# A diagonal state-space mixer that keeps its state at every fourth step, with its matrices made one mixer ahead

## The reference, cut to what matters

```python
u, q, k, v, r, glow = split(x @ w_in)            # x: 256 x 1024
# S5: 32 groups of 16 channels, 64 complex states each = 2048 states
abar = exp((lam_re + i*lam_im) * dt)             # one complex number a state
bbar = coef(abar) * b                            # 64 x 16 a group
x[t] = abar * x[t-1] + bbar @ u[t]               # linear scan over 256 steps
y    = Re(c @ x) + d_skip * u
g    = gelu(y);  y_s5 = g * sigmoid(g @ glu_w + glu_b)
# GLA: 4 heads, chunks of 64 tokens, q_dec, k_inv, k_end, three chunk states
o    = head_norm(att @ v + q_dec @ state) * silu(r)
out  = concat(y_s5, o) @ w_out
```

## Time and profile before

| | us |
|---|---|
| median of 3 runs | 1386.54 (1384.82 to 1388.08) |
| time of the profiled execution | 1389.13 |
| its span | 1387.4 |
| PE busy in the span | 1313.1 |
| DVE busy | 582.8 |
| POOL busy | 133.8 |
| second mixer, first useful matmul (L723) to end of its last (L631) | 673.36 to 862.58 |

### The profile page before, as it was taken

One profiled execution on the slowest core, in us unless ns is written; L12 is line 12 of the kernel. 1 busy time (PEld: TensorE's weight loads), 2 busy tenths in 40 slices (PEclk: granted clock), 3 DMA queues, 4 the chain that ended last, 5 costly groups with the idle time before them and its releaser, 6 DMA issues. The chain is left out here.

```text
span 1387.4 us, 16354 instructions
## 1 busy us (share of the span) xinstructions
PE 1313.1 (95%) x6324; PEld 700.8 (51%) x6324; DVE 582.8 (42%) x1145; ACT 192.0 (14%) x317; POOL 133.8 (10%) x123
## 2 busy tenths in 40 slices
PE   7999999999999999999956779999999999999997
PEld 5864645445445445454743444645445445445443
DVE  4235623333333333333778963523333333333334
ACT  3130201111111111111120120211111111111111
POOL 1000100000000000000777830100000000000000
PEclk9999999999999999999977869999999999999999
DMA  6525949999999999997311017789999999999992
GB/s 195 164 94 204 408 169 409 422 422 422 422 422 422 422 422 421 422 422 287 110 53 61 31 61 281 304 331 418 422 421 422 422 421 422 422 422 422 422 421 84
DMA packets 75547, 448.87 MB, mean 324 GB/s; under 512 B 9456, under 2 KB 10496, under 8 KB 25600
## 3 DMA queue, kind: packets, MB, share of 16 engines
q1 hardware_dynamic: 75520, 448.52, 79.5%
HBM read 447.44 MB, written 1.05 MB: 323 GB/s over the span
## 5 line engine op out<-in xcount | busy, mean ns | idle before, releaser
L1030 PE MATMUL bank<-expert_weights,hiddenT 128*64 128x512 f32 x1024 | 233.8, 598 | 0.0
L1003 PE MATMUL bank<-expert_weights,hT 128*64 128x512 f32 x1024 | 225.3, 592 | 0.0
L1003 PE MATMUL bank<-expert_weights,weight_ring 128*64 128x512 f32 x1024 | 225.2, 592 | 0.0
L1699 DVE TENSOR_TENSOR hidden<-silu_gate,bank 128x256 f32<-128x256 f32 x64 | 27.0, 421 | 333.3 <-ACT silu_gate L1206 333.3
L1003 PEld LDWEIGHTS bank<-expert_weights,hT 128*64 128x64 f32 x1024 | 73.4, 137 | 146.6 <-issue 146.6
L1003 PEld LDWEIGHTS bank<-expert_weights,weight_ring 128*64 128x64 f32 x1024 | 73.6, 137 | 146.2 <-issue 146.2
L956 PE MATMUL bank<-onehot_r,h_top 128*128 128x256 f32 x544 | 134.1, 289 | 0.0
L1030 PEld LDWEIGHTS bank<-expert_weights,hiddenT 128*64 128x64 f32 x1024 | 67.8, 136 | 117.7 <-issue 109.6
L956 PE MATMUL bank<-onehot_r,h_low 128*128 128x256 f32 x544 | 127.1, 277 | 0.0
L937 PE MATMUL bank<-y_top,onehotT_r 128*128 128x512 f32 x264 | 111.8, 423 | 0.0
L937 PE MATMUL bank<-y_low,onehotT_r 128*128 128x512 f32 x264 | 104.5, 396 | 0.0
(11 more groups left out here) (322 smaller groups left out, 1236.3 us busy)
## 6 DMA issues: line engine op xcount, KB each, us to landing
expert_weights<-in_exp_w_gate SPq DMA_DIRECT2D x128, 1024.0 KB, 10.9
expert_weights<-in_exp_w_up SPq DMA_DIRECT2D x128, 1024.0 KB, 13.3
expert_weights<-in_exp_w_down SPq DMA_DIRECT2D x128, 1024.0 KB, 12.6
weight_ring<-in_w_in_even SPq DMA_DIRECT2D x6, 2048.0 KB, 10.2
weight_ring<-in_w_out SPq DMA_DIRECT2D x4, 2048.0 KB, 7.4
weight_ring<-in_w_in_odd SPq DMA_DIRECT2D x4, 2048.0 KB, 9.4
ln_w<-in_ln_w SPq DMA_DIRECT2D x4, 512.0 KB, 13.4
ln_b<-in_ln_b SPq DMA_DIRECT2D x4, 512.0 KB, 14.6
```

What stands on the lines that cost most here:

```text
L1003: last = nc.tensor.matmul(bank[6][a * CAP:(a + 1) * CAP, :].rearrange("p (w f) -> p w f", w=2), xq[:, c, s0:s0 + CAP], ew_gu(2 * u + a, c) ...
L1030: last = nc.tensor.matmul(bank[b][a * CAP:(a + 1) * CAP, :], hm[:, j, a * CAP:(a + 1) * CAP], ew_d(2 * u + a)[:, j, half * 512:(half + 1) ...
L1699: nc.vector.tensor_tensor(hslot[:, :], sg[:, :], bank[6][:, DE:2 * DE], ALU.mult)\
```

## The change

S5 works with four phases. For each state the kernel keeps the state only at steps 3, 7, 11, ..., that is 64 of 256, and advances it by the fourth power of `abar`. The inputs of four steps enter a state through matrices `bbar * abar^k`, k = 0 to 3 (`bt`); the outputs at the steps between leave it through `c * abar^k` (`cmat`); what an input does to outputs fewer than four steps later goes through small matrices made by `pe_direct` from `bbar` and `cmat` (`direct`). The parts:

- In `mix0`: `dve_s5_powers` (30 small operations on 128x16 data) and `pool_s5` (six doublings to 64 steps, then `bbar`), one more transpose `G` on TensorE with a copy on ScalarE, a store of `G` to memory, four loads that spread its rows over 32 partitions each, `dve_s5_matrices` (12 operations of 1024 elements, 1 of 512 and 6 of 1536), and two stores of 2 MB and 3 MB (`s5_b`, `s5_c`).
- On SyncE's queue in `mix0` the loads `q0`, `v0`, `gb0` now stand behind the store of `G` and the four spreading loads, and `o0` behind the two stores.
- In `mix1`: `s5_c` (3 MB) and `s5_b` (2 MB) are loaded. The first waits only for the first of `moe0`'s four last accumulations. `pe_direct` takes the place of the second `keep_clock`. The inputs are 128 matmuls of 32x128 weights on 64 columns, then `qk`, `v`; VectorE does all tiles at once on 64 steps; then 24 direct matmuls and 128 output matmuls of 128x32 weights on 64 columns. GpSimd has only memsets and the mask.
- The order behind: `att`, keys, `r` half, `U`, `r` half, gate, `o`, output projection `a` (S5), head transposes, projection `b` (GLA).
- `moe1` may load three experts ahead (before: one), behind the same wait for `o1`.

```diff
-            for name in ("xb0", "k0", "q0", "v0", "gb0", "o0", "out_b0", "out_a0"):
+            for name in ("xb0", "k0"):
                 ring_load(sp, ring_no[name])
+            for dst, src in ((s5_room[:, 6144:7168], A["c_odd"]), (s5_room[:, 4096:5120], A["bt_odd"]),
+                             (xg[...], A["b_odd"])):
+                sp.dma_start(dst, src).then_inc(M1["raw_in"], 16)
+            sp.wait_ge(*B0.read("G"))
+            sp.dma_start(A["s5_rows"], hslot[:, P:2 * P]).then_inc(M1["rows"], 16)
+            sp.wait_ge(M1["rows"], 16)
+            for j in range(4):
+                src = A["s5_rows"].rearrange("(a j q) s -> j a (q s)", j=4, q=4)[j]
+                sp.dma_start(s5_room[32 * j:32 * j + 32, 0:4096].rearrange("p (a n) -> p a n", a=8),
+                             src.partition_broadcast(32)).then_inc(M1["rows"], 16)
+            for name in ("q0", "v0", "gb0"):
+                ring_load(sp, ring_no[name])
+            sp.wait_ge(M1["bt"], 2)
+            sp.dma_start(A["s5_b"], s5_room[:, 0:4096]).then_inc(M1["stored"], 16)
+            sp.wait_ge(M1["tables"], 1)
+            sp.wait_ge(M1["ct"], 1)
+            sp.dma_start(A["s5_c"], s5_room[:, 6144:12288]).then_inc(M1["stored"], 16)
+            for name in ("o0", "out_b0", "out_a0"):
...
 # TensorE, mix1
+            for q in range(4):
+                for w in range(2):
+                    for r in range(4):
+                        for j in range(4):
+                            rows = slice(32 * j, 32 * j + 32)
+                            last = nc.tensor.matmul(B.tile(f"bu{j}")[:, (2 * q + w) * S5C:(2 * q + w + 1) * S5C],
+                                                    W["bt"][rows, 3 - r, w, q, :], phases[rows, q, r, :],
+                                                    start=(r == 0), stop=(r == 3))
...
+            pe.wait_ge(M1["states"], 1)
+            for q in range(4):
+                out = ...
+                for r in range(4):
+                    k, lag = (0, 0) if r == 3 else (r + 1, 1)
+                    for w in range(2):
+                        for j in range(4):
+                            last = nc.tensor.matmul(out[32 * j:32 * j + 32, r, lag:], W["cmat"][:, k, w, 4 * j + q, :],
+                                                    W["m1"][:, w, 4 * j + q, 0:S5C - lag], start=False, ...)
...
 # VectorE, mix1: in place of 16 scan_tile
+            for j in range(4):
+                nc.vector.tensor_tensor(W["m1"][:, :, 4 * j:4 * j + 4, :], bu, c, ALU.mult)
+                nc.vector.tensor_tensor(W["m2"][:, :, 4 * j:4 * j + 4, :], bu, sn, ALU.mult)
+            nc.vector.tensor_tensor(W["m1"][:, 0], W["m1"][:, 0], W["m2"][:, 1], ALU.add)
+            nc.vector.tensor_tensor(W["m1"][:, 1], W["m1"][:, 1], W["m2"][:, 0], ALU.subtract)
+            for w in range(2):
+                last = nc.vector.tensor_tensor_scan(flat(W["m2"][:, w]), flat(W["mag"]), flat(W["m1"][:, w]), 0.0, ...)
+            nc.vector.tensor_tensor(W["m1"], W["m2"], c, ALU.mult)
+            nc.vector.tensor_tensor(W["m2"], W["m2"], sn, ALU.mult)
+            nc.vector.tensor_tensor(W["m1"][:, 0], W["m1"][:, 0], W["m2"][:, 1], ALU.subtract)
+            nc.vector.tensor_tensor(W["m1"][:, 1], W["m1"][:, 1], W["m2"][:, 0], ALU.add).then_inc(M1["states"], 1)
...
 # ScalarE, mix1: between the copies of hT and the copy for `low`
+            for j in range(4):
+                last = nc.scalar.copy(W["direct"][rows, :, :, 32 * j:32 * j + 32], ...)
...
-        EARLY_SLOTS = (2, 1)
+        EARLY_SLOTS = (2, 3)
```

More of the change, by code:

```diff
@@ L191, in build @@
                   "expd hstat hstd yhead y_lru out_full")
-        M1 = sems("m1_", "cols params full done_a done_d zeros dt ang sine coef bbar step_re step_im cneg "
-                  "gla_ln gla_last decays ki masked hstat hstd yhead z x y5 gelu5 y_s5 "
-                  "out_full")
+        M1 = sems("m1_", "cols params full done_a done_d zeros dt ang sine coef powers raw_in rows tables "
+                  "bbar bt ct stored c_in b_in direct gla_ln gla_last decays masked hstat hstd yhead states y_s5 "
+                  "gelu5 out_full")
         for l in range(2):
@@ L497, in pool_bbar @@
[L497 to L508 removed]
+            pool.wait_ge(*B1.read("att1"))
@@ L630, in pe_out @@
                     for m in range(4):
-                        last = nc.tensor.matmul(bank[2 * t + n][:, :], mixT[:, m + 4 * first, t * P:(t + 1) * P],
+                        last = nc.tensor.matmul(bank[2 * t + n][:, :], mixT[:, m0 + m, t * P:(t + 1) * P],
                                                 w[:, m, n * 512:(n + 1) * 512],
@@ L745, in pe_mix1 @@
-            pe.wait_ge(*B.read("bT1"))
-            def inputs(tiles):
-                for i in tiles:
-                    q, j = i // 4, 32 * (i % 4)
-                    B.wait_free(pe, f"bu{i}")
-                    for w in range(2):
-                        last = nc.tensor.matmul(B.tile(f"bu{i}")[:, w * SEQ:(w + 1) * SEQ], W["bT"][j:j + 32, w, q, :],
-                                                W["uT"][j:j + 32, q, :], start=True, stop=True)
-                    last.then_inc(B.full_sem, 1)
@@ L757, in outputs @@
-            def outputs(tiles):
-                for i in tiles:
-                    q, j = i // 4, 32 * (i % 4)
-                    pe.wait_ge(M1["x"], i + 1)
-                    for w in range(2):
-                        last = nc.tensor.matmul(bank[6 + q // 2][j:j + 32, (q % 2) * SEQ:(q % 2 + 1) * SEQ],
-                                                W["craw"][:, w, i, :], W["x"][:, i % 4, w, :], start=(w == 0), stop=(w == 1))
-                    last.then_inc(M1["y5"], 1)
-            inputs(range(0, 4))
+            pe.wait_ge(M1["b_in"], 16)
@@ L797, in pe_mix1 @@
             last.then_inc(B.full_sem, 1)
-            outputs(range(6, 9))
-            inputs(range(10, 13))
+            ring_arrived(pe, "r1")
+            token_major(pe, B, ring_view("r1"), "r", 0)
             pe.wait_ge(*B.read("keT"))
@@ L1120, in act_mix1 @@
             act_copies(act, B, "T2", hT[:, 4:6, :])
+            act.wait_ge(M1["direct"], 1)
+            act.wait_ge(*B.full("K"))
+            for j in range(4):
+                rows = slice(32 * j, 32 * j + 32)
+                last = nc.scalar.copy(W["direct"][rows, :, :, 32 * j:32 * j + 32],
+                                      B.tile("K")[rows, 0:384].rearrange("p (q k c) -> p q k c", q=4, k=3))
+            last.then_inc(B.done["a"], 1)
             act.wait_ge(*B.full("low"))
@@ L1124, in act_mix1 @@
                 act_copies(act, B, f"u{i}", W["uT"][:, 2 * i:2 * i + 2, :])
-            for w in range(2):
-                act.wait_ge(*B.full(f"bT{w}"))
-                nc.scalar.copy(W["bT"][:, w, :, :], B.tile(f"bT{w}")[:, :].rearrange("p (q n) -> p q n", q=4))\
-                  .then_inc(B.done["a"], 1)
             act.wait_ge(*B.read("ga"))
```

440 lines of the change are left out of this document (247 added, 193 removed), and 9 rows, old and new, of tables (B0, odd_jobs).

## The result

The changed kernel takes 1343.12 us (median of 4 runs, 1341.52 to 1345.51) against 1387.22 for the kernel before on the same chip (4 runs, 1384.82 to 1388.08): ratio 0.9689, 95% interval 0.9672 to 0.9706. The forecast was 1347.5. Its profiled execution took 1342.36, span 1340.7; the span before was 1387.4, so 46.7 us went where 39.0 were forecast. They split into 54.9 less in the second mixer (forecast 45.1) and 8.1 more in what lies ahead of it (forecast 6.1).

A forecast was written before the change was run, and what follows sets the result against it. TensorE sets the pace, with time to gain only in the mixers: second mixer 45.1 us less, first 6.1 more, so 39.0 less. Profiled 1389.1 becomes 1350.1, median 1347.5 us; range 1336 to 1368.

The forecast's parts named there:

- `q0` in time: Rival, first mixer: spreading loads run beside `q0`, the store is quick, stall and clock loss vanish: 1341.5 us, chance 8%.
- The start of `u`: Second mixer: `low` starts at 679.9 us, 5.0 late plus 1.5 for half clock, takes 3.5, then `u` starts.
- full clock from 680 on: Sign to look for in the second mixer: the granted clock at 1.00 from 680 us on.
- Inputs: Second mixer: 128 input matmuls, 256 records in four row groups at 0.05 us, 12.8 us (bounds 9.2 to 29.4).
- Outputs: Second mixer: 128 output matmuls, 256 records at 0.045 us, 11.5 us (bounds 9.2 and 28.2).
- output loads don't overlap: Rival, second mixer: column groups use the same rows, each load 0.11 us, outputs 28.2 us: 1364 us, chance 14%.
- `qk` and `v`: Second mixer, behind the inputs: `qk` 14.4 us with its wait, `v` 14.3 us, to 740.1.
- half clock in the small matmuls: Rival, second mixer: inputs, direct and outputs last 1.89 times as long, +26.5 us: 1374 us, chance 7%.
- VectorE behind the inputs: Second mixer: 19.4 us of VectorE work under 34.1 us of `qk`, `v` and direct matmuls, cover 14.7 us.
- stall 4.1 forecast: First mixer: `q0`, behind store, wait and spreading loads, lands at 49.6 us; TensorE stalls 4.1 us, plus 2.0 of lower clock.
- VectorE in the first mixer: First mixer: VectorE's S5 matrices take 25.6 us and end at 72.6 us.
- who waits: First mixer: `gate_cols`, and through its bank the second half of `v`, waits for the matrices; cover 9 us.

The follow-up runs named there:

- the second kernel of the start: Changed kernel with six idle matmuls ahead of the second transposes, `pe_direct` behind these, and `K` behind the `hT` copies in the bank list: 1335.8 us (0.9624).
- The experiment: Changed kernel with the 256 output records issued one column group after the other instead of four in turn: 1350.7 us (0.9749).
- `q0` ahead or between: Changed kernel with the load of `q0` issued ahead of the store of `G`, or between that store and its wait: 1342.7 us (0.969) and 1339.6 us (0.9657).
- the last kernel: Kernel with all gaining edits together (1326.6 us), and `v`'s 2 MB for the second mixer loaded only when the input matmuls are done: 1324.4 us (0.9554).

## Why the prediction was right, and where its terms were off

The direction and the mechanism held: the second mixer's tables and the waits for GpSimd went, TensorE became the only bound there, the expert stages only shifted. The sum was 7.7 us too small a gain, out of errors of opposite sign, and that it came out this near is in part luck: the small matmuls were priced 11.7 us too high, the first mixer and `qk` with `v` 4.9 too low, and 1.5 came back by the clock. The measured 1343.1 lies nearer to the 1341.5 of the rival "`q0` in time", whose stall did not vanish, than to 1347.5.

1. **The start of `u`, right by its sum alone.** `u` was forecast 22.1 us behind VectorE's first statistics (679.9 + 3.5 - 661.35) and starts 22.08 behind them (691.53 - 669.45). But `low` started 2.8 earlier than forecast and then ran at half clock, 6.37 for 3.5, against the forecast's sign of full clock from 680 on. The missing `keep_clock` and the wait for the copies of `K` were both in the forecast; that both can be avoided the second kernel of the start shows (`u` 6.1 earlier in its trace, 7.3 us in its median).
2. **Inputs: 12.8 forecast, 8.9 measured** (7.7 without the gap). I took 0.05 a record from rows with three row groups in flight; four give 0.031, where one alone takes 0.1065.
3. **Outputs: 11.5 forecast, 3.74 measured, below my lower bound of 9.2. This is the term that failed most.** I took 0.045 from weight loads and from 256-column records, and both ends of the range came from rows of long records or of loads at the start of a burst. The experiment gives 0.0446 for one group at a time, so that in effect I had priced the outputs as if the groups waited for each other; that my 0.045 is so near to it is chance. The rival "output loads don't overlap" (28.2) is refuted. The Trainium skill (TensorE: Matmul & The Clock Gate, "What overlaps and what doesn't") says that a weight load overlaps matmuls in flight only where the row group differs. For the inputs 0.1065 a record in one row group and 0.031 in four fit that, but don't prove it. Records on the full array take 0.12 with 64 columns (5.77 / 48 at L799) and 0.11 with 129:

```profile
109.75 0.39 PE L729 MATMUL bank<-expert_weights,decay_scores 128*128 128x129 f32 x2
109.98 0.39 PE L730 MATMUL bank<-expert_weights,decay_scores 128*128 128x129 f32 x2
```

The pairs start 0.23 us apart. If a load waited there for the matmul in flight, the 65 further columns would show, 0.05 us at the pace of the large matmuls (0.22 for 256 columns); so loads of 128 columns that follow each other at about 0.11 are the likelier limit in one row group. For the outputs the runs differ from it: all records use the same rows, and loads and matmuls alternate. If each load waited for the matmuls in flight, no two matmuls could overlap, and the order of the groups would change nothing; it changes 11.42 to 3.74 us. So loads of one column group run under the matmuls of the others; the measurement decides.
4. **`qk` and `v`: 28.7 forecast, 30.1 measured**, from the clock behind the gap in the inputs. The rival "half clock in the small matmuls" came true in a small part: 0.5 us of gap and 1.4 of clock here, 0.4 to 1.6 and up to 2.8 in the other traces, not 26.5.
5. **Everything behind the outputs** was forecast at 60.5 (757.0 to 817.5) and took 61.1 (754.68 to 815.82), with another gap of 0.85 at L819, which ends 2.2 us behind the start of an instruction packet at 754.5.
6. **VectorE behind the inputs:** 19.4 forecast, 18.7 measured. No wait for `states`, as said; the cover is 17 where 14.7 was forecast.
7. **The first mixer: stall 4.1 forecast, 8.55 measured; clock 2.0 forecast, 2.75 measured.** The form of the step held (store, wait, spread, then `q0`), its size did not: 2 MB of spreading loads at 217 GB/s are 9.7 us, not the 6.7 at 313. I had taken the rate of a load with long rows for one that spreads rows over 32 partitions. Of the sum of 11.3, 9.56 are left at the output projection.
8. **VectorE in the first mixer** ended at 73.75 (forecast 72.6). That "who waits" was right: `gate_cols` became the next limit as soon as `q0` was in time. Of the 9 us of cover 6.1 were the stall and clock that I had just added; with `q0` ahead or between, the spread rows come later too, and nothing is left. So the rival "`q0` in time" had its own price wrong: that order alone gives 0.4 to 3.5 us, not 6.
9. **The extra early experts** are worth nothing, as said.

So: second mixer 9.8 better (inputs 3.9 and outputs 7.8 better, `qk` with `v` 1.4 and the rest 0.5 worse), first mixer 3.5 worse (9.56 for 6.1), and 1.5 back by the clock in the router's matmuls, which belongs to neither.

## What to carry to other kernels

Small matmuls that use a quarter of the array are to be issued so that the quarters take turns, row groups and column groups alike; priced from a row of one group of the same shape, divided by the number of groups in turn (0.011 and 0.027 a record here, measured 0.0146 and 0.031), not by rows with other shapes. When a stall is lifted, compute the cover of everything behind it again: cover measured beside a stall contains the stall. A stage of hundreds of short instructions wants no large load started beside it. And a wait ahead of a stage is better removed than filled: idle matmuls in the first of two waits left the clock low behind the second.

## What the runs showed of the hardware that I had not expected

- Instructions can come late. Packets of 0.02 MB come on the instruction queue, about 3.6 us apart in the inputs of the last kernel; with 2 MB of weights landing beside them TensorE stood still for up to 1.6 us in eleven of the twelve kernels with that load, always until 2.3 to 2.4 us behind the packet's start, and not in the kernel without the load. The Trainium skill (Runtime: NRT & Kernel Launch, "Instruction fetch mechanics") says that blocks of 16 KiB, 256 instructions, are fetched while the one before is executed, and that this is hidden behind the pace of dispatch. Size and pace agree roughly with these traces (0.02 MB; 512 instructions in 7.8 us, a packet each 3.6 us); that it is hidden does not hold here beside a large load.
- Four column groups in turn give 3.05 times the rate of one (11.42 to 3.74 us), four row groups 3.5 times (0.1065 to 0.0306 a record).
- A load that spreads rows over 32 partitions fills the DMA engines (share 1.06) at 216 to 218 GB/s, the weight load of `q0` behind it at 388 in the changed kernel (1.05).
- The same instructions at the same place run at either clock level without an edit that bears on them: the router's 16 records in 3.55 or 1.95 us, `low` in 5.2 to 5.3 or 6.2 to 6.4 behind the same waits. A difference of 1 to 2 us between two traces is to be looked for there first.
- Open: what decides between the two levels of `low`, and why the packet comes at 2.7 us in one trace and at 4.4 in another.
